# Expert routing of a two-layer diffusion backbone: logits from raw transposed rows, one-hot matrices per expert group, gather from the residual

## What is computed

```python
# x: the residual stream; one (shift, scale, gate) of its own per stream and layer
h   = rmsnorm(x, g_pre2) * (1 + scale) + shift
aff = softmax(h @ w_router)                  # 16 experts, per token
g, idx = top_k(aff.T, cap)                   # 32 tokens per expert and stream
xs  = h[idx]
hid = silu(xs @ w1) * (xs @ w3)              # 1024 -> 1024, per expert
y   = (hid @ w2) * g
out = zeros_like(h).at[idx].add(y)           # then post-norm, gate, residual
```

## Time and profile before

| | |
|---|---|
| median of 3 runs | 2035.05 us (2030.12 to 2037.28) |
| the profiled execution, its own time | 2038.31 us |
| its span, first to last instruction | 2036.5 us |
| mean granted clock of TensorE, as a share of 2.4 GHz | 0.923 |
| PE busy | 1740.6 us, 85% |
| DVE, ACT, POOL busy | 468.3, 318.7, 85.3 us |
| read from memory | 522.70 MB |

### The profile page before, as it was taken

One profiled execution on the slowest core, in us unless ns is written; L12 is line 12 of the kernel. 1 busy time (PEld: TensorE's weight loads), 2 busy tenths in 40 slices (PEclk: granted clock), 3 DMA queues, 4 the chain that ended last, 5 costly groups with the idle time before them and its releaser, 6 DMA issues.

```text
span 2036.5 us, 21586 instructions
## 1 busy us (share of the span) xinstructions
PE 1740.6 (85%) x9237; PEld 883.8 (43%) x9237; DVE 468.3 (23%) x980; ACT 318.7 (16%) x750; POOL 85.3 (4%) x138
## 2 busy tenths in 40 slices
PE   6999999999997998979888799999976767667765
PEld 2656454344475332424222376667863323222222
DVE  2145144211115111112120514253122101011102
ACT  4113243100023010101000312242020000000001
POOL 5000110000003000000000000110000000000000
PEclk9999999999999999999999899999996777777776
DMA  9310104645317899999999912114634999999996
GB/s 348 96 42 21 16 0 186 210 142 206 125 63 264 368 421 421 421 422 421 421 421 422 382 60 63 16 54 133 210 121 198 421 421 420 421 421 420 421 421 255
DMA packets 130666, 525.15 MB, mean 258 GB/s; under 512 B 9886, under 2 KB 73532, under 8 KB 75276
## 3 DMA queue, kind: packets, MB, share of 16 engines
q1 hardware_dynamic: 127884, 520.47, 64.6%
q0 software_dynamic: 2688, 3.32, 0.9%
HBM read 522.70 MB, written 1.05 MB: 257 GB/s over the span
## 4 chain that ended last, share of the span: by engine, by line
PE 56%; DMA 37%; DVE 5%; ACT 1%; issue 1%; SPq 0%; DVEq 0%; ACTq 0%
DMA ring<-in_w_e_dram 35%; PE ps L666 13%; PE ps L926 9%; PE ps L1071 6%; PE ps L932 4%; PE ps L962 4%; PE ps L890 3%; PE ps L852 2%; PE ps L595 2%; PE ps L1024 2%; PE ps L1093 2%; PE ps L768 2%; PE ps L1051 1%; DMA ring<-in_w_mod_dram 1%; PE ps L601 1%; PE ps L874 1%
## 5 line engine op out<-in xcount | busy, mean ns | idle before, releaser
L1071 PE MATMUL ps<-ring,arena 128*32 128x256 f32 (+1 forms) x3072 | 415.3, 520 | 135.1 <-DMA ring<-in_w_e_dram 132.2
L1071 PEld LDWEIGHTS ps<-ring,arena 128*32 128x32 f32 (+1 forms) x3072 | 132.4, 131 | 402.9 <-DMA ring<-in_w_e_dram 227.3
L1093 PE MATMUL ps<-ring,arena 128*32 128x256 f32 (+1 forms) x1536 | 231.5, 586 | 73.5 <-DMA ring<-in_w_e_dram 71.2
L926 PE MATMUL ps<-arena,ring 128*128 128x512 f32 (+1 forms) x576 | 192.4, 487 | 0.0
L666 PE MATMUL ps<-arena,ring 128*128 128x512 f32 (+1 forms) x480 | 175.2, 523 | 1.4 <-DVE arena L1571 1.4
L1093 PEld LDWEIGHTS ps<-ring,arena 128*32 128x32 f32 (+1 forms) x1536 | 72.4, 144 | 229.4 <-issue 116.4
L1401 ACT ACTIVATE arena<-ps 128x512 f32<-128x512 f32 (+1 forms) x32 | 15.7, 490 | 832.0 <-PE ps L1071 832.0
L926 PEld LDWEIGHTS ps<-arena,ring 128*128 128x128 f32 x576 | 108.7, 190 | 77.9 <-issue 70.4
L1756 DVE COPY arena<-ps 32x512 f32<-32x512 f32 (+1 forms) x128 | 70.9, 554 | 282.6 <-PE ps L1093 281.3
L666 PEld LDWEIGHTS ps<-arena,ring 128*128 128x128 f32 x480 | 90.2, 190 | 82.5 <-issue 76.6
L1131 ACT ACTIVATE arena<-ps 128x256 f32<-128x256 f32 (+4 forms) x152 | 74.0, 493 | 221.5 <-PE ps L962 69.2
(11 more groups left out here) (188 smaller groups left out, 1289.6 us busy)
## 6 DMA issues: line engine op xcount, KB each, us to landing
ring<-in_w_e_dram SPq DMA_DIRECT2D x384, 1024.0 KB, 17.9
ring<-in_w_mod_dram SPq DMA_DIRECT2D x48, 1024.0 KB, 8.9
ring<-in_w_in_dram SPq DMA_DIRECT2D x44, 1024.0 KB, 10.3
ring<-in_w_out_dram SPq DMA_DIRECT2D x8, 1024.0 KB, 9.9
arena<-in_w_br_ml_dram SPq DMA_DIRECT2D x8, 512.0 KB, 6.4
arena<-in_w_br_mla_dram SPq DMA_DIRECT2D x8, 256.0 KB, 3.9
arena<-in_w_br_na_dram SPq DMA_DIRECT2D x8, 256.0 KB, 4.7
arena<-in_rpb_dram POOLq DMA_DIRECT2D x16, 96.0 KB, 4.1
```

Of the source, the lines that this page charges most:

```text
L926: mm = pe.matmul(ps[:, u % 3, tq], wg[:, k, cols], hT[:, k, tq], start=k == 0, stop=k == KD - 1)
L1071: mm = pe.matmul(ps[M * j:M * j + M, m, 0:NW], XST[e // GROUP % 2][:, kk, e % GROUP, 0:M], w[:, k, j * NW:(j + 1) * NW], start=kk == 0, st ...
L1093: mm = pe.matmul(ps[M * j:M * j + M, 3, 0:NW], lhs, w[:, k, j * NW:(j + 1) * NW], start=kk == 0, stop=kk == KD - 1)
```

## The change

- **Logits.** No row is normalised and no modulated transpose is made. X itself is turned, chunk by chunk (`turn_rows`), and copied out raw into `XT`, the lower four feature blocks by ACT, the upper four by DVE. POOL has multiplied the router weights by the scale ahead of time (`wrs`) and by the shift (`wsh`), into the room of the MLA query weights, which are not needed by then. A product of ones with `wsh`, summed by DVE over the blocks, gives the shift's share of the logits (`shl`). Products and group sums are made per chunk; DVE multiplies the sums by the token's reciprocal root and adds `shl` (`logits_of`). ACT takes the sum of squares of a chunk of X ahead of its last copy of the next chunk's projection.
- **Modulation group 4.** Three of its eight products come behind the logits, five behind the affinities' transposes. Its row on DVE comes behind the first one-hots, its transposes and copy behind the gates of group 0.
- **One-hots.** `hot` holds one group of four experts at a time, 128 columns for each stream and half. ACT scales it by the reciprocal root into `Sr`; POOL multiplies it by the affinities into `Sg`. DVE's `one_hot(g + 1)` stands at the start of group g and waits for both.
- **Gather** multiplies raw X, with a column stride of two, by `Sr`.
- **Gate rows of the second half** are spread and copied in the second expert.
- **POOL** loads layer 1's router, gate and MLA weights earlier, and those of modulation group 5 later.

The core of the diff:

```diff
@@ pe @@
-                    for k in range(KD):
-                        mod_product(4, k)
-                norm_turn(l, 2, xn2, L.chunks)
+                for si, s in enumerate(L.streams):
+                    mm = pe.matmul(ps[:, 6, si * P:(si + 1) * P], ones[:, :], wsh[:, s, :, :].rearrange("p k e -> p (k e)"),
+                                   start=True, stop=True)
+                for j in range(L.nt):
+                    turn_rows(j)
+                    if L.nt == 4 and j == 0:
+                        continue
+                    for i in ([0, 1] if L.nt == 4 and j == 1 else [j]):
+                        logit_parts(i)
+                        logit_sums(i)
+                if l == 0:
+                    for k in range(3):
+                        mod_product(4, k)
...
                 mm.then_inc(sem("affT_tr"), 1)
                 if l == 0:
-                    pe.wait_ge(sem("mod_col"), 5)
-                spread_gate(2)
+                    for k in range(3, KD):
+                        mod_product(4, k)
...
-                                    mm = pe.matmul(ps[:, 4 + 2 * s + b, i * P:(i + 1) * P], xn2[:, 2 * s + c2, k * P:(k + 1) * P],
-                                                   Ssel[:, si, c2, g * P:(g + 1) * P], start=c2 == 0, stop=c2 == 1)
+                                    mm = pe.matmul(ps[:, 4 + 2 * s + b, i * P:(i + 1) * P], X[:, 2 * s + c2, paired(k)],
+                                                   Sr[:, si, c2, :], start=c2 == 0, stop=c2 == 1)
@@ act @@
+                        if j and nb == 3:
+                            act.wait_ge(sem("x_post1"), before("x_post1", l) + j)
+                            norm_stat(2, L.chunks[j - 1], junk_y)
...
+                if nt == 4:
+                    rows_turned(0)
+                    rows_turned(1)
+                    parts_taken(0)
+                    parts_taken(1)
+                    rows_turned(2)
+                    parts_taken(2)
+                else:
+                    rows_turned(0)
+                    parts_taken(0)
+                own(act.activation(junk_y, X[:, tl, :], ACT.Square, accum_out=stat[:, tl:tl + 1]))
+                rows_turned(nt - 1)
+                rstd(stat[:, tl:tl + 1], stat[:, tl:tl + 1], D).then_inc(sem("n2_rstd"), 1)
+                parts_taken(nt - 1)
@@ dve @@
-                for j, t in enumerate(L.chunks):
-                    post(1, j, t, Ym, G1, tmp1)
-                    if j:
-                        norm_rows(l, 2, j - 1, L.chunks[j - 1], xn2)
-                norm_rows(l, 2, nt - 1, L.chunks[-1], xn2)
-                norm_lat(l, 2, h2T)
-                if l == 0:
-                    mod_row(4)
+                for j, t in enumerate(L.chunks[:-1]):
+                    post(1, j, t, Ym, G1, tmp1)
+                for j in range(nt // 2):
+                    rows_turned(j)
+                post(1, nt - 1, L.chunks[-1], Ym, G1, tmp1)
...
+                def one_hot(g):
+                    if g:
+                        dve.wait_ge(sem("weighted"), before("weighted", l) + g)
+                        dve.wait_ge(sem("rows_scaled"), before("rows_scaled", l) + 2 * ns * g)
...
+                one_hot(0)
+                if l == 0:
+                    mod_row(4)
@@ pool @@
+            def router_weights(l):
+                for s in layers[l].streams:
+                    for kh in range(2):
+                        own(pool.tensor_tensor(wrs[:, s, ks, :], wrt[:, ks, :], sc.to_broadcast([P, 4, 2 * N_EXP]), ALU.mult))
+                        own(pool.tensor_tensor(wsh[:, s, ks, :], wrt[:, ks, 0:N_EXP], sh.to_broadcast([P, 4, N_EXP]), ALU.mult))
```

204 lines of the change are left out of this document (141 added, 63 removed).

## The result

The changed kernel takes 2018.68 us (median of 7 runs, 2014.98 to 2025.18) against 2035.05: a ratio of 0.9928, 95% interval 0.9912 to 0.9944, 16.4 us less. The prediction said 2019.3, range 2013 to 2027. The profiled execution took 2019.38 us with a span of 2017.6, against 2038.31 and 2036.5.

A forecast was written before the change was run, and what follows sets the result against it. The weight stream sets both expert stages, so only the chain from output projection to first expert can shorten. 5.7 us in layer 0 plus 10.1 in layer 1 is 15.8; 2035.05 less that gives 2019.3 us, range 2013 to 2027.

The forecast's parts named there:

- Part 1: Ahead of the router: normalised rows and modulated transposes go; new DVE operations beside POOL's memset read PSUM, priced at plain duration.
- The rival of 2024 us: Memset blocks DVE's PSUM copies too: they wait 2.6 us in layer 0, 2.3 in layer 1; 7%.
- Part 2: From X complete to row maximum: only the last chunk remains to be turned; maximum 6.2 us sooner in layer 0.
- its two cases: Layer 1, X to row maximum: 10.1 us gained at the upper clock, 8.8 at the lower.
- Part 3: Layer 0: layer 1's modulation products move behind the logits, costing 0.7 us on the path and holding the ring's loads.
- Part 4: Ranks to gather: one-hots by group gain 1.2 us in layer 0, 0.5 in layer 1; gather's stride costs 1.0 and 0.5.
- PE and the ring are ready together: Layer 0's first expert: stream back at 661.3 us by PE, 660.9 by the ring; the later counts, gaining 5.7 us.
- Part 5: Expert stage: gate spreading, one mod turn, later groups' scalings and one-hots hide in PE's waits; price 0, uncovered 4 us.
- The clock rival: Router chains of both layers: clock falls early, nothing of layer 0's 5.7 us left, layer 1 8.8; time 2027, 13%.
- The rival in which PE becomes the bound in layer 0's experts: Clock falls while PE waits in layer 0's experts: 41 us an expert instead of 30.1; with three, 2052; 4%.

The follow-up runs named there:

- memset_late: Kernel before, with only POOL's memset of the accumulators moved behind the normalised rows of the second half: 2028.23 us, ratio 0.9966.
- memset_twice: Changed kernel with the memset of the accumulators done twice in each layer, 7.0 us instead of 3.5: 2022.76 us in one run.
- filled_both: Changed kernel with idle PE products between router steps in layer 1 and also in layer 0: 2015.31 us, ratio 0.9909.
- products_gaps: Changed kernel with layer 1's eight modulation products placed two behind turns of chunks 2 and 3, two in the softmax gap, four under top-8: 2018.63 us, ratio 0.9927.
- filled_l1: Changed kernel with idle PE products between router steps in layer 1 alone: 2018.39 us, ratio 0.9918.
- the second comparison: The unchanged changed kernel run once more against the kernel before: 2022.45 us, ratio 0.9941.

## Why the prediction was right, step by step

**Part 1, the row passes and the memset: right.** The longest DVE row pass went from 4.09 us to nothing, the copies beside the memset take 0.69, and no DVE row of the chain is over 1.28. memset_late shows the contention's price in the kernel before (2.3 and 3.2 us), memset_twice that the copies from PSUM don't meet it. The rival of 2024 us is out. The page "SBUF — State Buffer" of the Trainium skill ("Who interferes with whom") separates the two cases in the same way; the 4.09 against 0.75 us and the six copies of 691 or 692 ns agree with it.

**Part 2, behind the last chunk.** Layer 0: the maximum was to be 13.1 us behind the projection (637.2 against 624.1) and is 12.7; X is complete 6.1 us behind it, expected 5.9. Layer 1: 4.5 us behind X where 3.9 was said. The turn (1.23 against 1.2), the square pass, both copies and the scaling came out as priced. The two terms that were off are the products, 1.08 against 0.8, and their sum, 0.61 against 0.45: the clock fell in 1512 to 1514, between the turn and the products. At the upper clock, in layer 0, they take 0.65 and 0.40. The prediction gave 10.1 and 8.8 as its two cases and took the upper clock; the gain was 9.65, or 9.5 counted from the projection as those are, between them. The lower one was worked out wrongly: by its own terms (1.9, 1.3 and 0.8 against 1.2, 0.8 and 0.45) 8.6 would be left and not 8.8, and these terms are not doubled, as the text says.

**Part 3, the products: right.** Three end at 637.6 while the softmax's last step ends at 636.74: 0.84 lost, 0.7 said. The first expert load is issued 13.5 us behind the projection, 13.4 said. Five lie under the top-8 rounds. From the maximum to the one-hots it is 9.46 us instead of 8.71.

**Part 4, one-hots and gather.** From the start of the one-hots to the gather it is 1.75 us instead of 2.65: 0.9 gained where 1.2 was said. The one-hots are four of 0.23 as priced, but all four scalings on ACT (1.28 us for them) stand ahead of the gather and not only the last. In layer 1 0.3 instead of 0.5. The stride was sized wrong as well: 0.4 us at the upper clock instead of 1.0. The two misses cancel in part. That the gather runs mostly at the lower clock held: 10.5 and 9.2 us in layer 0, 6.0 and 6.3 in layer 1.

The first expert of layer 0 was to come 35.0 us behind the projection (659.1) and came 34.4 and 33.0 behind. That PE and the ring are ready together (661.3 and 660.9) is what decided most, and the runs bear it out: the share drops first in 658 to 660 us, 0.74, one microsecond behind the first expert, and taking either limit away alone moves nothing in the profiled executions (filled_both, products_gaps). Layer 0 gave 6.8 and 6.4 us against 5.7, layer 1 9.0 and 9.6 against 10.1.

**Part 5, price 0 in the expert stage: right.** PE is busy for 403.5 of 455 us where it was 400.7, and the stretch from the first expert to the last scatter is 470.7 and 472.5 against 471.3. In the changed kernel the stream sets this stretch, so the cleaner test is products_gaps, where PE does: 471.5.

**The clock rival, half right.** In layer 0 the clock stays at 1.00 from the projection to 644 us, through transposes and small products alone until 634.9; in layer 1 it falls 6 to 8 us behind the projection. The page "TensorE: Matmul & The Clock Gate" of the Trainium skill (Part 4) says that the full clock doesn't engage for transposes. The low clock that the prediction took from it for both chains didn't come in layer 0: 10 us of transposes and small products stand at 1.00 there (7.01 us busy in 624 to 634). But the clock was up when they began and they aren't transposes alone, so the page's sentence itself isn't tested. Layer 1 shows a fall for which no run here gives the rule. The price that the prediction set on the rival in layer 1, 1.3 us, is 0.45 so far as the maximum goes, but filled_l1 shows that the low clock costs 3 us by the first expert, the gather above all: 2 us. The prediction left this cost in its base, since the gather before ran mostly at the lower clock too.

**A rival's sum.** The rival in which PE becomes the bound in layer 0's experts doesn't add up as it stands: at 41 us instead of 30.1 three experts cost 32.7 us, which gives its 2052, but the sentence before says that the first such expert doesn't count. The rival didn't come (1.00 over 657 to 1112 us).

**What the sum didn't know.** The total was right within 1 us, but part of that is luck. Layer 0 gave 0.7 to 1.1 us more than said and layer 1 0.5 to 1.1 less, and the two misses cancel. And the total itself moves more than that: the profiled executions alone would have said 18.9, because 3 us of clock in untouched stretches fell to the kernel before, and the second comparison says 12.8.

## What to carry to other kernels

When two limits are ready together, each experiment on one of them shows no gain, and both must be moved to see either: here the idle products and the earlier ring loads gave 0 and 0 alone, 3 us together in layer 0's part, in profiled executions that can differ by 2. Cut the executions at marks that the change touches and compare only those stretches; the rest varied by more than the parts that were at issue. And before rewriting a chain to make it shorter, see whether one of its steps is only held up by a neighbour: letting one memset begin 2.5 us later, alone, brought 5.6 us, as much as a third of this gain. Before filling a wait, read its length in every layer: 2.8 us of idle products in a wait of 0.66 us cost 2.6.

## What the hardware showed

The granted clock falls behind the same 2.6 us gap on PE in some executions and not in others (3 of 12), and one such fall is worth 2.8 us here. Idle products that nobody reads held it at 1.00 through waits in which it otherwise falls: between layer 1's projection and its first expert it fell in all nine executions without them and in none of the four with them, and in the same stretch of layer 0 in all ten without and in none of the three with them. A gather of 64 at stride two took 7.8 us instead of 9.2 to 10.5, one of 32 took 4.0 instead of 6.0 to 6.4. Reading the gather's columns of X at stride two cost 6 ns a record, 7.70 against 7.31 us for 64.
